# First weights of eight stages loaded one stage ahead, and the recurrence's result kept in the input's tile

## What is computed

```
layer 0: hn = rms_norm(x) * (1 + scale) + shift
         zh, zq, zk, zv = split(hn @ e_w_in)
         y_h = x0 * (centred_fftconv(x1 * hv, filt) + x1 * hv * bias)   # from short_conv(zh)
         y_a = attention(rms_norm(zq), [cache_k, rms_norm(zk)], [cache_v, zv])
         x = x + gate * ([y_h, y_a] @ e_w_out)
         x = x + gate_f * expert_choice_ffn(norm(x), router_w, w_gu, w_down)
layer 1: z = hn @ r_w_in -> q, i, f_fw, f_bw, g    # 8 heads of 128
         o = gla_chunk_scan(forward) + flip(gla_chunk_scan(backward))
         x = x + gate * ((rms_norm(o) * silu(g)) @ r_w_out)
         x = x + gate_f * expert_choice_ffn(norm(x), router_w, w_gu, w_down)
return final rms_norm(x), new keys, new values, final scan states
```

## Time and profile before

| what | value |
|---|---|
| device time, median of 3 runs (lowest to highest) | 4476.14 us (4475.63 to 4477.32) |
| device time of the profiled execution | 4479.9 us |
| span of the profiled execution | 4478.1 us |
| mean granted TensorE clock (1.00 is 2.4 GHz, 0.50 is 1.2 GHz) | 0.941 |
| PE busy, share of the span | 3959.1 us, 88% |
| DVE, ACT, POOL busy | 1820.1, 1096.3, 156.8 us |
| moved by DMA | 616.30 MB |

### The profile page before, as it was taken

One profiled execution on the slowest core, in us unless ns is written; L12 is line 12 of the kernel. 1 busy time (PEld: TensorE's weight loads), 2 busy tenths in 40 slices (PEclk: granted clock), 3 DMA queues, 4 the chain that ended last, 5 costly groups with the idle time before them and its releaser, 6 DMA issues. The chain is left out here.

```text
span 4478.1 us, 55788 instructions
## 1 busy us (share of the span) xinstructions
PE 3959.1 (88%) x23797; PEld 3156.1 (70%) x23797; DVE 1820.1 (41%) x2978; ACT 1096.3 (24%) x2013; POOL 156.8 (4%) x152
## 2 busy tenths in 40 slices
PE   5798988989579999999699999999668299999996
PEld 1454455554169999999588888888644199999995
DVE  4324346752621111111278888888932611111112
ACT  1210024532110101110334554544422001010111
POOL 0000000000000000000000000000000000000000
PEclk8899988999789999999899999999889599999998
DMA  6201100013778888885310001010032478888884
GB/s 233 89 15 55 41 0 1 1 62 108 286 224 263 262 263 262 259 256 167 93 31 28 28 27 32 16 32 19 7 149 99 130 231 261 266 260 265 260 257 166
DMA packets 521950, 616.30 MB, mean 138 GB/s; under 512 B 16076, under 2 KB 466248, under 8 KB 521065
## 3 DMA queue, kind: packets, MB, share of 16 engines
q1 hardware_dynamic: 502216, 543.33, 37.3%
q0 software_dynamic: 16448, 58.73, 5.1%
q10 hardware_dynamic: 3040, 10.68, 0.6%
HBM read 558.86 MB, written 53.84 MB: 137 GB/s over the span
## 5 line engine op out<-in xcount | busy, mean ns | idle before, releaser
L1449 PEld LDWEIGHTS moe_pgu<-step_hnT,mw_w 128*128 128x128 f32 x8192 | 1118.1, 191 | 16.5 <-issue 16.5
L1449 PE MATMUL moe_pgu<-step_hnT,mw_w 128*128 128x160 f32 x8192 | 1125.8, 300 | 3.4 <-ACT step_hnT L1489 3.4
L1513 DVE TENSOR_TENSOR moe_hT<-moe_sg,moe_pgu 128x160 f32<-128x160 f32 x256 | 82.0, 321 | 1028.2 <-PE moe_pgu L1449 971.6
L1461 PE MATMUL moe_pol<-mw_w,moe_hT 128*128 128x256 f32 x2048 | 457.5, 381 | 2.3 <-DVE moe_hT L1513 1.0
L1691 PE MATMUL rec_pz<-step_hnT,rec_w 128*128 128x256 f32 x1920 | 425.2, 381 | 10.0 <-DMA rec_w<-in_r_w_in 8.0
L1461 PEld LDWEIGHTS moe_pol<-mw_w,moe_hT 128*128 128x128 f32 x2048 | 383.2, 190 | 59.0 <-DVE moe_hT L1513 10.0
L1691 PEld LDWEIGHTS rec_pz<-step_hnT,rec_w 128*128 128x128 f32 x1920 | 362.9, 191 | 58.9 <-DMA rec_w<-in_r_w_in 8.3
L1500 ACT ACTIVATE moe_sg<-moe_pgu 128x160 f32<-128x160 f32 x256 | 77.8, 304 | 1317.6 <-PE moe_pgu L1449 1317.6
L1695 PE MATMUL rec_pz<-rec_w,step_hnT 128*128 128x256 f32 x1280 | 284.8, 381 | 15.1 <-ACT rec_zg L1766 15.1
L1695 PEld LDWEIGHTS rec_pz<-rec_w,step_hnT 128*128 128x128 f32 x1280 | 241.5, 191 | 49.7 <-ACT rec_zg L1766 17.9
L1721 PE MATMUL rec_pg<-rec_ring 128*128 128x128 f32 x1600 | 198.4, 283 | 49.8 <-DVE rec_AT L2007 18.5
(11 more groups left out here) (316 smaller groups left out, 4391.6 us busy)
## 6 DMA issues: line engine op xcount, KB each, us to landing
mw_w<-in_moe_w_gu SPq DMA_DIRECT2D x256, 1024.0 KB, 11.0
mw_w<-in_moe_w_down SPq DMA_DIRECT2D x128, 1024.0 KB, 13.7
mod_w_ring<-in_mod_w SPq DMA_DIRECT2D x24, 1024.0 KB, 14.3
mw_w<-in_mod_w SPq DMA_DIRECT2D x24, 1024.0 KB, 14.3
rec_w<-in_r_w_in SPq DMA_DIRECT2D x40, 512.0 KB, 4.0
scratch_xm<-op_x ACTq DMA_DIRECT2D x20, 512.0 KB, 2.6
scratch_xn<-op_xn POOLq DMA_DIRECT2D x20, 512.0 KB, 5.2
hin_w<-in_e_w_in SPq DMA_DIRECT2D x12, 512.0 KB, 6.8
```

The source lines that it names most:

```text
L1449: m = nc.tensor.matmul(pgu[2 * (f % 2) + part][:, :], w[:, j, k, (f % 2) * P:(f % 2 + 1) * P], ring[:, k, e % 8, :], start=(k == 0), stop= ...
L1461: m = nc.tensor.matmul(pol[q // 2][:, (q % 2) * SW:(q % 2 + 1) * SW], hT[:, k, 0:CL], w[:, 8 + q, k, :], start=(k == 0), stop=(k == KD - 1))
L1513: nc.vector.tensor_tensor(hT[:, f, :], sg[:, f % 2, :], pgu[2 * (f % 2) + 1][:, :], ALU.mult).then_inc(multiplied, 1)
```

## The change

Each of the eight first loads gets a place in SBUF at a fixed offset and semaphores that outlive the stage (class `Early`). The stage before issues the loads at the end of its own list on SP (or, in `attention`, as the whole list). What is left in the stage itself are the later loads. In detail:

- n0 issues the six loads of the first two weight groups of hin; hin issues the first two `fwd` of cv, behind its own last weights; cv issues six of the eight qkv weights (k = 2 to 7) when PE has done all forward transforms; qkv issues k = 0 and 1 itself, and PE takes the order 2 to 7, 0, 1.
- att issues the eight weights and the two gate rows of op0; op0 and op1 issue the router's weight of rt0 and rt1 ahead of their own x tiles; n2 issues the five weights of rec's first head.
- rec issues, when all projections and head 6 are done, the eight weights and two gate rows of op1. Three weights lie in half of `zc`, five in the place of rec's own weights. When heads 0 to 6 have been written to DRAM, it reads them back into `hnT`, which no projection needs any more. The last head's result is written by DVE into `hnT` directly, and neither written to DRAM nor read back.
- One scope with semaphores (around rec and op1) is new, and the outermost scope has semaphores now: two more clears with a meeting of the engines, one behind op1, one at the end.

```diff
+class Early:
+    def __init__(self, nc, sem, name, shape, offset, sems, dt=F32):
+        self.t = nc.alloc_sbuf_tensor_at(name, shape, dt, offset=offset)
+        self.loaded = [sem(f"{name}_in{i}") for i in range(sems)]
...
             for t in range(NT):
                 sp.dma_start(x[:, t, :], x_dram(t)).then_inc(x_in[t], 16)
+            next_loads(sp)
...
-            for i in range(4):
-                if i >= 2:
-                    sp.wait_ge(mm, 9 * (i - 1))
-                for part in range(3):
...
+            for i in range(2, 4):
+                sp.wait_ge(mm, 9 * (i - 1))
+                load_hyena_w(sp, A, early, i)
+            for n in range(2):
+                load_conv_forward(sp, A, fwd, n)
...
             sp.wait_ge(h_mm, NUNIT - 1)
             sp.dma_start(inv1_last, A["k_inv_l"][1, :, 4:6]).then_inc(i2_in, 16)
+            sp.wait_ge(u_mm, NUNIT)
+            for k in QKV_ORDER[0:6]:
+                load_qkv_w(sp, A, qkv_w, k)
...
+QKV_ORDER = [2, 3, 4, 5, 6, 7, 0, 1]
...
-            for k in range(KD):
-                sp.dma_start(w[:, k, :], A["e_w_in"][0, k * P:(k + 1) * P, 3 * HW:]).then_inc(w_in[k], 16)
+            for k in QKV_ORDER[6:]:
+                load_qkv_w(sp, A, early, k)
...
+def load_out_w(sp, w, w_in, w_dram, ks):
+    for k in ks:
+        sp.dma_start(w(k), w_dram[k * P:(k + 1) * P, :]).then_inc(w_in[k], 16)
...
-            for k in range(KD):
-                sp.dma_start(w[:, k, :], w_dram[k * P:(k + 1) * P, :]).then_inc(w_in[k], 16)
-                if lhs_dram is not None:
-                    sp.dma_start(lhs(k), lhs_dram[k]).then_inc(l_in[k], 16)
-            for c in range(2):
-                sp.dma_start(gate[:, c, :], S["mod_dram"][layer, c:c + 1, 2 * D:3 * D].broadcast_to([P, D])).then_inc(g_in, 16)
+            next_loads(sp)
             for t in range(NT):
...
-            sp.dma_start(w[:, :, :], A["router_w"][layer].rearrange("(k p) e -> p k e", p=P)).then_inc(w_in, 16)
             if mod:
                 mod.load_weights(sp)
...
             for h in range(RH):
-                for j, part in enumerate((0, 2, 3, 1, 4)):
-                    if h:
+                if h:
+                    for j in range(5):
                         sp.wait_ge(z_mm, NP_STEPS * (h - 1) + (NZU * (j + 1) if j < 3 else NP_STEPS))
...
+                        load_rec_w(sp, A, early, h, j)
...
+            sp.wait_ge(z_mm, NP_STEPS * RH)
+            sp.wait_ge(yT_ready, 3 * (RH - 1))
+            next_loads(sp)
+            sp.wait_ge(y_out, 16 * (RH - 1))
+            for h in range(RH - 1):
+                sp.dma_start(hnT[:, h, :], y_dram[h]).then_inc(yr_in[h], 16)
...
-                pool.wait_ge(yT_ready, 3 * (h + 1))
-                pool.dma_start(y_dram[h], ring[:, 1, :]).then_inc(y_out, 16)
+                if h + 1 < RH:
+                    pool.wait_ge(yT_ready, 3 * (h + 1))
+                    pool.dma_start(y_dram[h], ring[:, 1, :]).then_inc(y_out, 16)
             pool.wait_ge(fin_out, 32 * RH)
-            pool.wait_ge(y_out, 16 * RH)
...
+                    dst = r1 if h + 1 < RH else hnT[:, h, :]
```

More of the change, by code:

```diff
@@ L331, in _, with load_hyena_w, load_conv_forward, hyena_in @@
                 m.then_inc(tr, 1)
-def hyena_in(nc, A, S, hnT, x0, u, uT):
+def load_hyena_w(sp, A, early, i):
+    for part in range(3):
+        c0 = part * HW + i * P
+        sp.dma_start(early.t[:, i % 2, :, part, :],
+                     A["e_w_in"][0, :, c0:c0 + P].rearrange("(k p) n -> p k n", p=P)).then_inc(early.loaded[i % 2], 16)
+def load_conv_forward(sp, A, early, n):
+    if n == 0:
+        sp.dma_start(early.t[:, 0, 0, :, :, 0:96], A["k_fwd_c"].rearrange("p (a r f) -> p a r f", a=2, r=2)).then_inc(early.loaded[0], 16)
+    else:
+        sp.dma_start(early.t[:, n % 2, :, :, :, :].rearrange("p k a r f -> p (k a r f)"), A["k_fwd_l"][n - 1]).then_inc(early.loaded[n % 2], 16)
+def hyena_in(nc, A, S, hnT, x0, u, uT, early, fwd):
     NPS, NTR, NZ = 5, 3, 3
@@ L583, in _ @@
         def _(sp):
[L584 to L592, removed]
+            sp.dma_start(inv_c[:, :, :, :].rearrange("p a r m -> p (a r m)"), A["k_inv_c"]).then_inc(ic_in, 16)
+            for n in range(2, NUNIT):
+                sp.wait_ge(h_mm, n - 1)
+                load_conv_forward(sp, A, early, n)
             sp.dma_start(inv0[:, :, :], A["k_inv_l"][0]).then_inc(i0_in, 16)
@@ L749, in qkv_in @@
         sb, ps, sem = scope(nc, ctx, "qkv")
-        w = sb("w", [P, KD, QW + 2 * KW])
+        w, w_in = early.t, early.loaded
         z = sb("z", [P, 2, QW + KW])
@@ L1078, in out_proj_norm @@
         pst = ps("pst", [P, D])
[L1079 to L1082, removed]
+        mm, products, gated, squared, v_steps, inverted, rooted, scaled, tr, hn_out = (sem(n) for n in (
+            "mm products gated squared v inverted rooted scaled tr hn_out").split())
         x_ins, stored = [sem(f"x_in{i}") for i in range(NB)], [sem(f"stored{i}") for i in range(NB)]
@@ L1582, in rec_order, with load_rec_w, recurrence @@
     return o
-def recurrence(nc, A, S, hnT, y_dram, out_state):
+def load_rec_w(sp, A, early, h, j):
+    part = (0, 2, 3, 1, 4)[j]
+    sp.dma_start(early.t[:, :, j, :], A["r_w_in"][0, :, part * D + h * RD:part * D + (h + 1) * RD]
+                 .rearrange("(k p) n -> p k n", p=P)).then_inc(early.loaded[j], 16)
+def recurrence(nc, A, S, hnT, y_dram, out_state, early, zc, yr_in, next_loads):
     with ExitStack() as ctx:
@@ new lines, in build_step, with load_hin, load_op @@
+            cv_fwd = Early(nc, sem, "cv_fwd", [P, 2, 4, 2, 2, P], EARLY["cv_fwd"], 2)
+            qkv_w = Early(nc, sem, "qkv_w", [P, KD, NH * HD + 2 * NKV * HD], EARLY["qkv_w"], KD)
+            op_w, gate = Early(nc, sem, "op0_w", [P, KD, D], EARLY["op0_w"], KD), Early(nc, sem, "op0_gate", [P, 2, D], EARLY["op0_gate"], 1)
+            ow = lambda k: op_w.t[:, k, :]
+            def load_hin(sp):
+                for i in range(2):
+                    load_hyena_w(sp, A, hin_w, i)
+            def load_op(sp):
+                load_out_w(sp, ow, op_w.loaded, A["e_w_out"][0], range(KD))
+                load_gate(sp, S, gate, 0)
@@ L2167, in build_step @@
+                attention(nc, A, S, qT, kT, v, ya, *pp, load_op)
+            out_proj_norm(nc, A, S, "op0", ow, op_w.loaded, gate, lambda k: (yh if k < 4 else ya)[:, k % 4, :], None,
+                          x_tile(A["x_prompt"], A["x_sample"]), rows(W["xm0"]), 0, hnT, W["xn"],
+                          lambda sp: load_router_w(sp, A, router_w, 0))
         idx = [sb("idx0", [CAP[0], NE], U32), sb("idx1", [CAP[1], NE], U32)]
```

126 lines of the change are left out of this document (69 added, 57 removed).

## The result

The changed kernel takes 4420.5 us (median of 4 runs, 4415.1 to 4423.5) beside 4476.7 us for the kernel before in the same measurement: a ratio of 0.9873, 95% interval 0.9861 to 0.9884. Measured a second time, unedited, it takes 4426.3 us (4423.7 to 4428.2) beside 4479.3 us, 0.9884 (0.9867 to 0.9900). The medians are 56.2 and 53.0 us apart; 56.7 was forecast. The profiled execution of the first measurement is its fastest, 4415.1 us with a span of 4413.3, so the two profiles are 64.8 us apart. Which stages hold them is the first question to the experiments.

What follows compares the result with a forecast made beforehand. PE was taken as the bound inside stages, with DMA waits ahead of its first rows in eight. Starts, clock terms and op1, less two clears, summed to 56.7 us: 4476.14 − 56.7 = 4419.4 us, range 4413 to 4438.

Steps and rivals of the forecast that it cites:

- The starts: Seven stages but op1: each gains PE's first row minus SP's first row minus 0.1 us, from 2.3 to 8.9.
- B: At every start, PE's sequencer gets under way later than SP's, a wait the loads hid; 6.2 us lost, 4425.6, chance 0.10.
- E: The early loads' queue is held until the stage's end, starts stay; time within 0.2% of before, chance 0.03.
- the bound of 0.78 for each start: If each of eight starts comes 0.78 us later, as DVE's first row in hin suggests, 6.2 us is lost.
- Covers: The stage before has time to hide the early loads: 12 to over 300 us, about 106 in rec.
- Rival A: In n0 and n2 early loads share engines with x tiles; at worst 9.0 us each, 18 lost, 4437.4, chance 0.08.
- Rival C: Gains at cv, rt0, rt1 and rec return as waits in work PE doesn't bound; 17.9 us, 4437.3, chance 0.05.
- Rival D: Moved rec_w and zc lengthen rec's DVE instructions, DVE becomes rec's bound; at 8% 71 us, 4490, chance 0.02.
- op1: First token tile waits for the seam alone; second tile's product at 3319.2 instead of 3336.11, 16.9 us gained.
- The extra clear: Two more clears with meetings of the engines cost 0.5 us each, between 0 and 0.85, 1.0 in all.
- The clock terms: First 6 us of hin, qkv, op0, rec run at full clock after shorter idle: 2.3, 2.5, 2.5, 2.1 us.
- Attention: No gain entered for attention; its otherwise idle SP only takes over op0's ten load issues.

Runs made afterwards that it cites:

- before_warm: Kernel before, with eight identity transposes that nobody reads added in each of attention's first seven pairs, nothing of the change: 4468.9 us, ratio 0.9983.
- warm_all: Changed kernel with unread identity transposes in attention's first seven pairs and at six more of PE's waits: 4407.8 us, 0.9841 of the kernel before.
- op1_h7: Changed kernel, but head 7 goes through DRAM again, written at rec's end and read back by op1: 4425.8 us.
- n2_w_first: Changed kernel, but n2 asks for rec's five first weights ahead of its x tiles instead of behind them: 4427.8 us.

## Why the prediction was right, and where it was not

**The starts** (8.9 + 3.0 + 3.2 + 3.5 + 2.3 + 6.3 + 4.2) came within 0.1 us each, hin's once the stages ahead of it are taken off, and so they did in the second profile. That says less than it seems: forecast and table take the wait from the same profile of the kernel before, so the agreement shows what is left of it, 0.05 us for the 0.1 allowed, and not that the wait is the same in every execution. In before_warm, where these starts are as before, rt0's is 3.22 us instead of 2.41 and rt1's 2.41 instead of 4.34. With 0.05 left, rivals B and E are gone, and so is the bound of 0.78 for each start: at hin, cv and rec PE is idle for 1.7 us in all, meeting included. The Trainium skill ("Runtime: NRT & Kernel Launch", section "Instruction fetch mechanics") says that a taken branch whose target isn't among the pages already fetched waits for a DMA to fetch it; none of the eight seams shows such a wait, with PE 0.05 to 0.21 us behind SP.

**Covers** held: hin's six loads took SP 16.19 us to issue behind the x tiles, not 8.74, but ended at 136.6, and n0 grew by nothing. Rival A is excluded for the change; its price for n2 was 9.4 us, close to the 9.0 that three other loads had given. Rival C falls: in the first profile no stage behind the starts of cv, rt0 and rt1 became longer by more than 0.12 us; in the second the stretch behind rt1's start is 1.0 longer, far from the 17.9. Rival D falls, and its price had little ground: 71 us more leave DVE at 961, under PE's 1015.66. The line of the earlier trace rows now takes

```profile
L2028 DVE TENSOR_TENSOR rec_ring<-rec_ring,l_zc x64: 814/820/826, 2204.7 to 3203.5; 128x640 f32<-128x640 f32 x64
```

**op1** was sized as a whole, 16.9, and measured 17.5 and 15.9. Which of the two it is goes with the clock of op1's first 6 us: in seven profiles the stretch is 32.1 us at 0.50 (three), 30.5 at 0.75 or 0.76 (three) and 29.4 at 1.00.

**The extra clear** behind op1 shows in these rows, the last of ACT before rt0 and before rt1:

```profile
1115.25 2.90 ACT L1197 ACTIVATE step_hnT<-op_pst,step_modcol 128x128 f32<-128x128 f32 x8 [2.13 <-PE op_pst L1152]
...
3402.33 2.90 ACT L1197 ACTIVATE step_hnT<-op_pst,step_modcol 128x128 f32<-128x128 f32 x8 [2.12 <-PE op_pst L1152]
```

From their ends to SP's next row it is 0.77 and 1.25 us, where both were 0.88 in the kernel before: 0.48 for the clear, 0.5 forecast. The one at the end was not measured alone.

**The clock terms** are the step that was mis-sized: "also gain 6 × (1 − clock), if the shorter gap leaves the clock up". In the first profile the clock at the start stayed up in all four stages, as said (in the second not in qkv). But only hin (2.47 for 2.3) and op0 (2.66 for 2.5) kept the gain. In qkv 0.79 of 2.5 was left and in rec 0.74 of 2.1: PE has another wait soon behind the start, and there the clock fell. Windows with that wait, qkv and then rec, in the kernel before:

```profile
545.92:555.92 10.00, 6.73 (x28) 4.22 (x27) 3.22 (x7) 3.30 (x9) 0.00 (x0) 1.00 0.03 9
...
2222.07:2232.07 10.00, 8.12 (x38) 6.84 (x37) 1.21 (x1) 9.90 (x9) 0.00 (x0) 1.00 0.01 3
```

and in the changed one:

```profile
527.18:537.18 10.00, 6.73 (x24) 3.92 (x23) 3.22 (x7) 3.30 (x9) 0.00 (x0) 0.83 0.05 15
...
2180.10:2190.10 10.00, 8.13 (x33) 6.72 (x32) 3.23 (x3) 8.95 (x9) 0.00 (x0) 0.90 0.00 0
```

PE's idle time is the same to 0.01 us, and the clock is not: 1.00 before, 0.83 and 0.90 after. The 3.28 us gap that I took as evidence that short gaps leave the clock up kept it in the kernel before and lost it in the changed one. That this wait ate qkv's gain is shown by warm_all, which fills it with 16 transposes. The clock stays up behind it, and inside qkv it is 123.99 us, 2.46 less than before and so the whole of the 2.5:

```profile
527.30:537.30 10.00, 8.46 (x44) 5.86 (x43) 3.22 (x7) 3.31 (x9) 0.00 (x0) 1.00 0.05 15
```

In rec it is shown less well. In op1_h7 and n2_w_first the same wait, unfilled, ran at 1.00 and rec took 1102.5 us instead of 1105.3; but there the clock also stayed up at the place of a second fall that the first profile has (0.66 at 2345 to 2350). So a wait of this length decides nothing by itself; what decides was not found.

**Attention** was given nothing, rightly on the whole, but it varies by 7 us from run to run (328.2 to 335.6) and belonged in the range with both signs. The forecast's 56.7 against 56.2 and 53.0 therefore is partly luck: with attention's part taken out of both kernels it is 52.0, inside the range. And in the table the 3.1 us missing inside qkv and rec are set off by stretches that were given nothing: 1.07 ahead of hin, 1.07 in rt0, 0.64 in moe0 and n2. No run says what these are.

## What to carry to other kernels

The wait in front of a stage's first matmul can be read from a profile, and all but 0.05 us of it comes back when the load is issued a stage earlier behind that stage's own loads; but the wait itself differed by up to 1.9 us between two profiles with the same starts, so one profile is thin ground for a single start. Put ahead of n2's own loads, five weights cost n2 9.4 us. A gain that hangs on the granted clock should be entered only where PE then runs on without a wait, and with a lower bound of nothing even there (qkv in the second profile); a stage in which PE waits in every step should be given a range of its own. Weights that hide behind the first tile may not hide there together with its operands.

## What was not expected

- PE's clock stayed at 0.50 for some 40 us in attention, where PE waits for DVE and ACT in every pair, and came up within some 6 us of attention's start when these waits were filled with transposes that nobody reads. Filling them took 6.7 us off the median of the kernel before, and at six other places 7.7 to 9.2 more off the changed one.
- A wait of 3.28 us in qkv left the clock at 1.00 in the kernel before and was followed by a fall in the changed one (0.83 over the 10 us around it), with the same work on both sides.
- Two first weights of 512 KB cost different starts: 4.87 us from the issue of rec's to PE's first matmul, 3.53 for op0's. Four more weights in flight behind rec's first one added at most 0.69 us to its start.
